# Moving the steps of the paged decode attention by one page, regrouping its page waits, and moving one transpose of the feed-forward's first group

## The reference

```python
def page_step(carry, pages):                 # 16 pages of 128 tokens, for each of 8 sequences
    ckv = cache_ckv[layer, pages]            # 128 x 256 latents
    kpe = cache_kpe[layer, pages]            # 128 x 32 rotated keys
    k_nope, v = expand_kv(ckv, lp)           # k_nope is divided by its root mean square per head
    sc = attn_scores(q_nope, q_pe, k_nope, kpe)
    return online_update(carry, sc, v), None # maximum, exp, weighted sum
...
x = x + (silu(h @ w_gate) * (h @ w_up)) @ w_down
```

## Time and profile before

| | before |
|---|---|
| three runs, median | 1853.23 us (1852.12 to 1857.76) |
| the profiled execution | 1852.12 us, its span 1850.3 us |
| TensorE busy | 1762.0 us, 95% of the span |
| VectorE, ScalarE, GpSimd busy | 1028.0, 527.5 and 389.3 us |
| granted TensorE clock, mean | 0.989 |
| decode stage | 455 to 788 us |
| output projection | 788 to 923 us |
| first feed-forward group | from 923 us on |

### The profile page before, as it was taken

One profiled execution on the slowest core, in us unless ns is written; L12 is line 12 of the kernel. 1 busy time (PEld: TensorE's weight loads), 2 busy tenths in 40 slices (PEclk: granted clock), 3 DMA queues, 4 the chain that ended last, 5 costly groups with the idle time before them and its releaser, 6 DMA issues.

```text
span 1850.3 us, 27171 instructions
## 1 busy us (share of the span) xinstructions
PE 1762.0 (95%) x10268; PEld 1557.7 (84%) x10268; DVE 1028.0 (56%) x1659; ACT 527.5 (29%) x1040; POOL 389.3 (21%) x262
## 2 busy tenths in 40 slices
PE   7999898999999998889999999999999999999998
PEld 6999786667888887768798898998998998998886
DVE  5476885775888888756534334334334244244543
ACT  5202355555443443634321111111111111111111
POOL 2204693221655455513300000000000000000000
PEclk9999998999999999989999999999999999999999
DMA  6401000011421222120021111111111111112011
GB/s 188 125 6 39 14 1 0 1 34 33 138 53 52 64 62 66 46 97 1 8 84 46 34 44 37 44 45 45 45 45 45 45 45 45 45 68 77 29 43 41
DMA packets 108947, 91.89 MB, mean 50 GB/s; under 512 B 25571, under 2 KB 97792, under 8 KB 108845
## 3 DMA queue, kind: packets, MB, share of 16 engines
q1 hardware_dynamic: 106851, 89.63, 16.0%
q10 hardware_dynamic: 2002, 1.03, 0.2%
HBM read 84.73 MB, written 6.26 MB: 49 GB/s over the span
## 4 chain that ended last, share of the span: by engine, by line
PE 79%; DVE 8%; POOL 4%; ACT 3%; SPq 3%; issue 3%; DMA 1%; ACTq 0%; POOLq 0%; DVEq 0%
PE ps L1945 22%; PE ps L1947 22%; PE ps L1946 22%; POOL stats L751 2%; PE ps L2356 2%; PE ps L536 1%; PE ps L2187 1%; DVE arena L1410 1%; PE ps L2140 1%; SPq L624 1%; PE ps L1952 1%; DVE arena L1772 1%; PE ps L2144 1%; PE ps L2248 1%; DVE arena L1644 1%
## 5 line engine op out<-in xcount | busy, mean ns | idle before, releaser
L1945 PE MATMUL ps<-h_hi,w_hi 128*128 128x384 f32 (+1 forms) x1056 | 345.6, 327 | 0.0
L1946 PE MATMUL ps<-h_lo,w_hi 128*128 128x384 f32 (+1 forms) x1056 | 345.4, 327 | 0.0
L1947 PE MATMUL ps<-h_hi,w_lo 128*128 128x384 f32 (+1 forms) x1056 | 345.4, 327 | 0.0
L1867 DVE TENSOR_TENSOR gate_s<-gate_s,ps 128x384 f32<-128x384 f32 (+1 forms) x66 | 35.1, 532 | 337.8 <-PE ps L1947 337.8
L885 POOL TENSOR_TENSOR arena<-arena,mhalf 128x32 f32<-128x32 f32 x32 | 177.1, 5535 | 144.3 <-DVE arena L1776 144.3
L1946 PEld LDWEIGHTS ps<-h_lo,w_hi 128*128 128x128 f32 x1056 | 198.5, 188 | 0.5
L1945 PEld LDWEIGHTS ps<-h_hi,w_hi 128*128 128x128 f32 x1056 | 198.5, 188 | 0.5
L1947 PEld LDWEIGHTS ps<-h_hi,w_lo 128*128 128x128 f32 x1056 | 198.5, 188 | 0.0
L1879 DVE TENSOR_TENSOR arena<-arena,ps 128x512 f32<-128x512 f32 x187 | 128.3, 687 | 123.9 <-PE ps L1947 109.7
L530 POOL TENSOR_TENSOR stats<-stats,mhalf 128x1 f32<-128x1 f32 (+1 forms) x18 | 9.8, 543 | 888.4 <-DVE stats L520 888.4
L1945 PE MATMUL ps<-cw_hi,pT_hi 128*128 128x288 f32 x512 | 161.0, 314 | 10.2 <-DVE pT_lo L1691 9.4
(11 more groups left out here) (324 smaller groups left out, 3579.8 us busy)
## 6 DMA issues: line engine op xcount, KB each, us to landing
arena<-in_cache_ckv SPq DMA_DIRECT2D x128, 128.0 KB, 2.0
w_raw<-in_w_gate SPq DMA_DIRECT2D x22, 512.0 KB, 3.9
w_raw<-in_w_up SPq DMA_DIRECT2D x22, 512.0 KB, 5.1
arena<-in_x_prompt SPq DMA_DIRECT2D x16, 512.0 KB, 5.6
w_uk<-in_w_down SPq DMA_DIRECT2D x11, 512.0 KB, 3.5
w_uv<-in_w_down SPq DMA_DIRECT2D x11, 512.0 KB, 4.2
gw_raw<-in_w_in SPq DMA_DIRECT2D x8, 512.0 KB, 5.8
w_out<-in_w_out SPq DMA_DIRECT2D x1, 4096.0 KB, 13.3
```

Source lines behind the costliest of these rows:

```text
L1867: ch.link(nc.vector.tensor_tensor(gate_s[:, c], gate_s[:, c], ps[:, 2 * b + 1, 0:n], ALU.mult))
L1945: mm(out, left[0], right[0], start=start, stop=False)
L1946: mm(out, left[0], right[1], start=False, stop=False)
L1947: return mm(out, left[1], right[0], start=False, stop=stop)
```

## The change

In the decode stage the steps move, by page number within a sequence (of the sequence before, where marked *):

| step | before | after |
|---|---|---|
| `kpe_T` and `kpe_copy` | pages 1, 5, 9, 13 | pages 0, 4, 8, 12 |
| `kpe_scores` | 2, 6, 10, 14 | 1, 5, 9, 13 |
| `quad` 0, 1, 2 | 7, 11, 15 | 6, 10, 14 |
| `last_quad`* | 3 | 2 |
| `max_T`*, `row_of_max`* | 5 | 4 |
| `max_B`* (PE) | 6 | 5 |
| `shift`* (DVE) | 6 | 5 |
| `soft_exp`* (ACT) | 8 | 7 |
| `pv`* (PE) | 9 | 8 |
| `out_lat`* | 12 | 11 |
| mean for POOL | right behind the page sum of 3, 7, 11, 15 | same pages, behind the tap and the extra steps of the last sequence |

The page loads count up two semaphores (pages 0 to 7, and 8 to 15 with the own page), the rotary keys one of their own, which the first `kpe_T` of a sequence waits for. `h_T(8)` moves from ahead of the second block to ahead of the third.

```diff
-PART_PAGES = (0, 4, 8)
-PART_LOADS = (4 * 16, (4 + NPAGE) * 16, 8 * 16)
+PAGES_HALF = NPAGE // 2 * 16
...
-                        .then_inc(s_(f"pages_loaded{s}{min(g // 4, 2)}"), 16)
+                        .then_inc(s_(f"pages_loaded{s}{g // 8}"), 16)
...
-                        .then_inc(s_(f"pages_loaded{s}1"), 16)
+                        .then_inc(s_(f"kpe_loaded{s}"), 16)
...
-                    if g % 4 == 1 and n >= 4:
-                        kpe_copy(b if g > 1 else b - 1, g // 4 - 1 if g > 1 else 3)
+                    if g % 4 == 0 and n >= 1:
+                        kpe_copy(b if g else b - 1, g // 4 - 1 if g else 3)
...
-                    if g == 8 and b >= 1:
+                    if g == 7 and b >= 1:
                         soft_exp(b - 1, 1 - s)
...
                         .then_inc(s_("ksum_done"), 1)
-                    if g % 4 == 3:
-                        dve.wait_ge(s_("ksum_done"), NPAGE * b + g + 1)
-                        nc.vector.tensor_scalar(ms_k[:, 4 * q:4 * q + 4, :], ms_k[:, 4 * q:4 * q + 4, :], 1.0 / DN, EPS,
-                                                ALU.mult, ALU.add).then_inc(s_("msk_ready"), 1)
-                    if g in (7, 11, 15):
-                        quad(b, s, q - 1)
-                    if prev and g == 3:
-                        last_quad(b - 1, 1 - s)
-                    if prev and g == 5:
+                    if prev and g == 4:
                         row_of_max(b - 1, 1 - s)
-                    if prev and g == 6:
-                        shift(b - 1, 1 - s)
                     if g >= 7:
                         taps(1)
...
-                    if prev and g == 12:
+                    if g % 4 == 3:
+                        dve.wait_ge(s_("ksum_done"), NPAGE * b + g + 1)
+                        nc.vector.tensor_scalar(ms_k[:, 4 * q:4 * q + 4, :], ms_k[:, 4 * q:4 * q + 4, :], 1.0 / DN, EPS,
+                                                ALU.mult, ALU.add).then_inc(s_("msk_ready"), 1)
+                    if g in (6, 10, 14):
+                        quad(b, s, (g - 6) // 4)
+                    if prev and g == 2:
+                        last_quad(b - 1, 1 - s)
+                    if prev and g == 5:
+                        shift(b - 1, 1 - s)
+                    if prev and g == 11:
                         out_lat(b - 1, 1 - s)
...
-                if g in PART_PAGES:
-                    part = PART_PAGES.index(g)
-                    pe.wait_ge(s_(f"pages_loaded{s}{part}"), PART_LOADS[part] * (b // 2 + 1) + (16 if part == 2 else 0))
+                if g == 0:
+                    pe.wait_ge(s_(f"pages_loaded{s}0"), PAGES_HALF * (b // 2 + 1))
+                if g == NPAGE // 2:
+                    pe.wait_ge(s_(f"pages_loaded{s}1"), PAGES_HALF * (b // 2 + 1) + 16)
...
             def kpe_T(b, q):
+
+                if q == 0:
+                    pe.wait_ge(s_(f"kpe_loaded{b % 2}"), NPAGE * 16 * (b // 2 + 1))
...
+                    if g % 4 == 0 and n >= 1:
+                        kpe_T(b if g else b - 1, g // 4 - 1 if g else 3)
                     if g % 4 == 1 and n >= 4:
-                        kpe_T(b if g > 1 else b - 1, g // 4 - 1 if g > 1 else 3)
-                    if g % 4 == 2 and n >= 4:
-                        kpe_scores(b if g > 2 else b - 1, g // 4 - 1 if g > 2 else 3)
+                        kpe_scores(b if g > 1 else b - 1, g // 4 - 1 if g > 1 else 3)
...
+                    if b and g == 4:
+                        max_T(b - 1)
                     if b and g == 5:
-                        max_T(b - 1)
-                    if b and g == 6:
                         max_B(b - 1)
-                    if b and g == 9:
+                    if b and g == 8:
                         pv(b - 1, 1 - s)
...
                             if b == 1:
                                 pe.wait_ge(s_("x2_ready"), NT)
+                            if b == 2:
                                 h_T(NT - 1)
-                            if b == 2:
                                 pe.wait_ge(s_("c_hT"), NT)
```

More of the change, by code:

```diff
@@ L633, in load_kpe @@
                     sp.dma_start(kpe[s][:, g, :], A["cache_kpe"][0, bass.ds(page_of(b, g), 1)].rearrange("a p n -> (a p) n"))\
-                        .then_inc(s_(f"pages_loaded{s}1"), 16)
+                        .then_inc(s_(f"kpe_loaded{s}"), 16)
             def load_own(s):
                 sp.wait_ge(s_("page_set"), s + 1)
-                sp.dma_start(pages[s][0:NS, NPAGE, 0:KL], O[5][0].rearrange("b q n -> (b q) n")).then_inc(s_(f"pages_loaded{s}2"), 16)
+                sp.dma_start(pages[s][0:NS, NPAGE, 0:KL], O[5][0].rearrange("b q n -> (b q) n")).then_inc(s_(f"pages_loaded{s}1"), 16)
             load_own(0)
```

## The result

The changed kernel takes 1862.15 us (median of 14 runs, 1857.88 to 1867.84), the kernel before 1851.83 us on the same chips (14 runs, 1846.76 to 1857.76). The ratio is 1.0056, 95% interval 1.0043 to 1.0070: slower, by 10.3 us. The prediction had said 1856.7, with a range of 1851.5 to 1861, and called a change within 0.3% the likeliest; the measured time lies above its range. The changed kernel's profiled execution took 1863.92 us, with a span of 1862.1.

A forecast was written before the change was run, and what follows sets the result against it. It took the kernel as TensorE-bound, with PE and DVE waiting for each other in the decode stage. Terms 3.5 - 1.4 + 0.5 - 2.0 + 2.9 = +3.5 on the median 1853.23 gave 1856.7 us, range 1851.5 to 1861.

The forecast's parts named there:

- the third of the steady sequence: PE from `max_T` to `pv`: same work as before, 8.99 us less 0.2 to 0.4 of waiting; `pv` starts at +16.65.
- sixth: Sequence 6: its taps run out, PE sets its end, and `kpe_scores` now stands ahead of page 2: +0.5 us.
- Steps 1 and 2: GpSimd's later power makes DVE's last quad wait 1.4 us; `max_T` starts at +7.85 instead of +8.56, gaining 0.7.
- Steps 4 and 5: DVE rests 3.5 us ahead of page 9's sum, then runs 19.2 us; steady sequence 0.7 longer, +3.5 over five.
- `kpe_T`'s cover: PE's wait at page 0's `kpe_T` for page 14's quad: covered by 0.1 us, else up to 0.5 each sequence.
- Sequence 0 and the rotary keys: First sequence's uninterrupted DVE run starts 0.9 us earlier, and PE's wait for the rotary keys moves: together -1.4 us.
- Page loads: Loads start behind `pv`; a 0.4 us stall hides under DVE: cost 0, a late landing up to 1 us once.
- Sequence 7: Last sequence: `mix_scale` free of mean and quad, -0.9 us, and page 15 earlier, -1.1: together -2.0.
- `h_T(8)`: First feed-forward group: PE waits for `low_h` ahead of the third block, nothing covers it: +2.9 us.
- The one with the right sign: Rival: PE's waits at `kpe_T` break through (2.4 us) and `low_h` is slow (+1.5): 1860.6 us, chance 0.24.
- The page wait on PE's path: Rival: half-sequence page wait reaches PE's path, 1 us in each of six sequences: 1862.7 us, chance 0.06.
- The opposite one: Rival: last quad not held by GpSimd's power, steady sequence 41.1 us, whole 1848.3 us, chance 0.06.

The follow-up runs named there:

- two fills: Useless transposes on PE ahead of `max_T`: 14 in the changed kernel, 1855.67 us; 16 in the kernel before with longer `col_max`, 1858.88 us (unfilled 1868.21).
- fill14: Changed kernel with 14 extra identity transposes on PE directly ahead of its wait at `max_T` in sequences 1 to 7: 1855.67 us.
- mean_early: Changed kernel with the mean of every quad of pages put back directly behind the page sum: 1863.19 us.
- parts: Kernel before with page loads waited for in halves, rotary keys on their own semaphore, last sequence's `mix_scale` ahead of page 15's mean and quad: 1861.13 us.
- best2: best1 with `pv` back at page 9, the exponential at page 8 and `out_lat` at page 12: 1856.44 us.
- hT_back: Changed kernel with only `h_T(8)` put back ahead of the second block of the first feed-forward group: 1855.62 us.
- mean_tap: Changed kernel with only page 15's DVE order changed to page sum, mean, `out_latT`, then tap: 1849.92 us.
- before_late: Kernel before with `col_max` of sequences 0 to 6 made 1.2 us longer by a first maximum overwritten at once: 1868.21 us.
- best1: mean_tap with `h_T(8)` back ahead of the second block: 1844.95 us, ratio 0.9976 to the kernel before.

## Why the prediction was wrong

**The step that failed** is the third of the steady sequence: "PE from `max_T` to `pv` holds the same work as before ... It took 8.99 ... So `pv` starts at +16.65". The work is the same, but not the time, 10.38 us. I had put `max_T` at +7.85. PE's work ahead of it was over at 585.93, +7.56, and a page of 1.6 less is +5.96, so my own numbers held a stop of 1.9 us where there had been 1.00. I priced it by its own length and never asked what PE's clock would do behind it: the clock's fall is a term that the sum doesn't have. The longest stop of PE in the steady sequence of before was 1.42, and the clock held behind it. The fall cost 1.46 us in each sequence (44.03 less 42.57). The two fills show it: filled, the changed kernel's decode stage is 335.13 us, +0.8 on before, where the prediction's terms for that stage sum to 3.5 - 1.4 + 0.5 - 2.0 = +0.6. The missing term is the other 8.5. The same term is missing a second time, behind the wait for `low_h`, with 1.6.

The decode stage in four pieces, each from `max_T` to `max_T` (chunk_T 453.29, 449.76, 447.11; first `max_T` 503.21, 497.73, 495.16; sixth 712.51, 717.64, 707.92; seventh 754.28, 761.17, 749.98; `m_T` 787.64, 793.43, 782.24):

| piece | before | after | filled | forecast | after - before | filled - before |
|---|---|---|---|---|---|---|
| `chunk_T` to first `max_T` | 49.92 | 47.97 | 48.05 | -2.1 | -1.95 | -1.87 |
| five sequences | 209.30 | 219.91 | 212.76 | +3.5 | +10.61 | +3.46 |
| sixth | 41.77 | 43.53 | 42.06 | +0.5 | +1.76 | +0.29 |
| last `max_T` to `m_T` | 33.36 | 32.26 | 32.26 | -1.3 | -1.10 | -1.10 |

(`filled` is fill14. The forecast's -2.1 is sequence 0's -1.4 and the 0.7 by which `max_T` moves; -1.3 is what that leaves of sequence 7's -2.0.)

**Steps 1 and 2**, GpSimd and `col_max`: right. The last quad waits 1.32 us (1.4 forecast), and `max_T` is at +7.70 (7.85). The prediction's "5.54 in every one of 32 cases" is the median; the first, behind whose mean no quad stands, took 5.435. What I had not seen is why the power took 5.54 before and 5.43 after: mean_early shows that it is longer when an instruction with two inputs on DVE stands directly behind the mean.

**Steps 4 and 5**, DVE's rest ahead of page 9 and its run: right: 3.54 us (3.5), and 19.1 (19.2) in four of the five sequences. The one shown has 18.5 (602.83 to 621.36), by its short tap. **`kpe_T`'s cover** of 0.1 held well enough: PE waits there 5.7 us in twelve waits, and filled, with 5.7 in twelve as well, the sequence is as long as forecast.

**Sequence 0 and the rotary keys**: right together, not told apart. **Page loads**: 0 is right, but only with `pv` at page 8. The prediction wrote that they start behind `pv` and took `pv`'s place from the walk. parts and best2 show that a page later the same kind of wait costs about 9 us in all, most of it where the clock falls behind it.

**Sequence 7**: right in size, partly wrong in reason. I had given 0.9 to `mix_scale` coming free of the mean and the quad; moved alone in the kernel before, that gives nothing, since `kpe_T` ahead of `m_T` waits for the quad.

**`h_T(8)`**: the wait is the 2.9 forecast; with the half clock behind it the move costs 4.5.

The profiled executions give +9.3 and 4.5, 13.8 together, and the medians 10.3. The difference is not settled. Part of it may be that PE keeps its clock behind some of the stops, as it did behind one of six in the profiled execution of mean_early and two of six in that of hT_back; the executions of the changed kernel run from 1857.88 us at a mean granted clock of 0.987 to 1867.84 at 0.979.

**The rivals.** The one with the right sign had PE's waits at `kpe_T` and a slow `low_h`, which is not what happened. The page wait on PE's path, which would have given 1862.7, wasn't on it in the changed kernel, whose four waits of up to 1.0 lie under DVE; in parts and best2 it was. The opposite one, the last quad not held, would give a sequence of 41.1 us; mean_tap made that condition true and got 41.38.

## What to carry to other kernels

When a change makes TensorE's stop longer, price the stop and then the work behind it at half clock as well: here 0.7 us more of rest cost 1.46 us behind it, and 14 useless transposes took it back. A wait that another engine covers is not free either if the clock falls behind it. Where a GpSimd instruction is to start early, see what DVE runs in the moment in which it is issued: a 0.35 us copy ahead of the tap was worth 1 us of GpSimd. Before waits are merged into fewer groups, look at what starts the transfers; here the wait by halves was free with `pv` at page 8 and cost 9 us with it at page 9, most of it by the clock.

## What the runs showed of the hardware

- A stop of PE of 1.73 us at `max_T`, between two dense stretches, was followed by a granted clock of 0.52 for some 3 us; stops there of 0.8 to 1.4 were not, and 2.15 us gave the same as 1.73. It is not certain for each stop of 1.6 to 2.2 us: it fell behind all six in the kernel after, five of six in mean_early, four of six in hT_back and six of seven in before_late, and behind the one in best1, but not behind the one in mean_tap and the one in best2. Of the page waits of 2.2 to 3.1 us it fell behind four of six in parts and in best2. Nor is the length enough: at page 14 of the last sequence PE stands 1.66 to 1.82 us in twelve of the fourteen kernels, and the clock held in all. What decides is not shown.
- Nor does the fall come at once: behind some stops page 5 ran its twelve matmuls in 1.83 us instead of 2.8, so that only its last ones and what follows were slow.
- A power on GpSimd (32 values a partition) takes 5.43 us by itself, 5.54 with a 0.42 us two-input instruction of DVE directly behind its mean, and 6.40 with a 1.28 us tap there. In the other order, the power first, neither is longer (5.43 and 1.28 in mean_tap).
